# The second expert table of a PEER decoder layer in whole rows: 128 blocks of 8 KB per partition in place of 256 half rows, and two decode gather slots in place of three

## The chip, the cores and the metric

One core of one Trainium2 chip runs the kernel in one launch. The metric is the device time of one execution in microseconds (us); lower is better.

## The reference, cut to what matters

One decoder layer is computed for 256 prompt tokens (one sequence) and 64 decode tokens (8 sequences of 8), model width 2048, all in float32. Input projection, dilated attention and a short convolution, output projection and a layer norm come first. Then comes the part that the change touches, the PEER expert mixer: for each token, 8 heads choose 16 experts each out of 16384, and each expert is one row of 2048 floats in two tables, `peer_u` and `peer_v`.

```python
u = u_tab[et]                                    # (tokens, 128, 2048)
h = einsum('nd,nkd->nk', xt, u)
a = gt * gelu(h)                                 # gates from a softmax over the 16 scores
y = einsum('nk,nkd->nd', a, v_tab[et])
h = layer_norm(ALPHA * h + y)                    # ln2, then a gated per-layer embedding is added
```

## The kernel before, in words

Every engine has its own program, and semaphores order them. The stages are: input projection; attention and cache copies; output projection; query projection and expert selection (VectorE, "DVE"); the first expert table, one gathered row per prompt token and expert, 256 gathers of 128 rows (POOL issues them at L474, DVE multiplies and sums at L1102); building of the gate matrix; then the **second-table stage**, which the change rewrites; then layer norm 2, the gate projection and the output.

**The prompt's share of the second table is dense.** The gate matrix `gm` holds, for each of the 256 prompt tokens, a weight for each of the 16384 experts (zero for most), as 128 groups of 128 experts. So all of `peer_v` (128 MB) is streamed and multiplied: for group k, 128 rows of the table are a matrix of 128 x 2048, and the product with the 128 x 256 weights of the group is summed in PSUM over all 128 groups. To keep float32 precision both factors are split into a high part (rounded to fp32r) and a low part (the rest), and three matmuls are made of each product: hi x hi, hi x lo, lo x hi (`split_mm`, L1249 to L1251).

One group is worked in two pieces of 1024 columns (`PIECES = 256`, piece m = 2k + h):

- SP loads the piece into one of RL = 5 raw slots of 4 KB per partition (L427). It waits until PE has finished piece m - 5 (`vd_used`).
- ScalarE (ACT) makes the high part of the group's weights once per group (L688), then that of the piece (L694), in one of HS = 3 slots; it waits for piece m - 3 to be finished.
- DVE makes the low parts: of the weights once per group (L1181), of the piece (L1183), in place in the raw slot.
- PE makes 12 matmuls of 128x128 by 128x512 for the piece (2 token tiles x 2 column chunks x 3), so 24 per group, 3072 in all.

**The decode tokens' share is gathered beside it.** 64 decode tokens with two packed halves of their experts fill 128 partitions, so there are 64 gathers of the first table and 64 of the second, 1 MB each (8 KB per partition). POOL issues them (`decode_row`, L482) into DSLOT = 3 slots; a gather waits until DVE has used the slot (`d_free`). DVE uses one gather with one instruction over 128x2048 ("decode op" below): L1162 for the first table (a dot product), L1171 for the second (multiply and add). An order written out by hand says after which piece a decode op stands in DVE's program: `U_AT` puts op i behind piece 2i (64 ops over pieces 0 to 126, one per group), `W_AT` puts op 64 + i behind piece 134 + (27 i) // 16 (64 ops over pieces 134 to 240, 16 ops in 27 pieces).

```python
U_AT = {2 * i: i for i in range(64)}
W_AT = {134 + (27 * i) // 16: 64 + i for i in range(64)}
```

Memory: the gathers' slots lie at 152, 160 and 168 KB, the raw slots at 136 to 152 KB and 176 KB, the high slots at 180 to 192 KB. Near the end (m = 250) SP waits for the last decode op and loads the tokens back for the second layer norm: `x_tokens_again` (152 to 176 KB), one half MB folded from the decode sums and one load of 2 MB (L431). After the loop SP waits for `al_ok` (the last weights' low part) and loads the layer norm's gain and bias, two pieces of the gate weights and the embedding weights. In the code below the lines are those of the profile.

Of the kernel before, what the change touches and what calls it, by code (L numbers as in the profile page):

```python
# [35 lines left out]
DSLOT = 3  # L36
PAIRS = PH * TOPK
HALF = D // 2
EG = 4
GROUPS = 2 * 128 // EG  # L40
PIECES = 2 * NK
RL, HS, ST = 5, 3, 3
# [11 lines left out]
def decoder_step(nc, x_p, x_s, st_k, st_v, k_old, k_last, v_old, v_last, st_c, p_p, p_s, w_in, w_conv, w_out, ln1_g, ln1_b,  # L54
# [89 lines left out]
    ring = [at(f"expert_rows{i}", [128, D], f32, (152 if i < DSLOT else 96 - 24) * KB + i * 8 * KB) for i in range(NSLOT)]  # L144
# [3 lines left out]
    vrl = [at(f"v_raw{i}", [128, HALF], f32, (136 + 4 * i if i < 4 else 176) * KB) for i in range(RL)]  # L148
    vlo = [at(f"v_lo{i}", [128, HALF], f32r, (136 + 4 * i if i < 4 else 176) * KB) for i in range(RL)]
    vhi = [at(f"v_hi{i}", [128, HALF], f32r, (180 + 4 * i) * KB) for i in range(HS)]  # L150
# [76 lines left out]
    with ctx:  # L227
# [77 lines left out]
        GELU_AT = 130  # L305
# [5 lines left out]
        def _(sp):  # L311
# [104 lines left out]
            v_rows = v_tab.rearrange("(k p) (h c) -> p k h c", p=128, h=2)  # L416
# [22 lines left out]
            sp.wait_ge(vd_used, PIECES)  # L439
# [15 lines left out]
        def _(pool):  # L455
# [32 lines left out]
            for m in range(PIECES):  # L488
                if m in DECODE_AT and DECODE_AT[m] + DSLOT < 128:
                    decode_row(DECODE_AT[m] + DSLOT)  # L490
            pool.wait_ge(vd_used, PIECES)
# [5 lines left out]
        def _(act):  # L497
# [183 lines left out]
            for m in range(PIECES):  # L681
                k = m // 2
                if m == GELU_AT:
                    dots_gelu(2, 0, 64)
                if m % 2 == 0:
                    if k >= ST:
                        act.wait_ge(vd_used, 2 * (k - ST) + 2)
                    A(ghs[:, k % ST, :], gm[:, :, k], ACT.Copy).then_inc(ah_ok, 1)  # L688
                if m >= HS:
                    act.wait_ge(vd_used, m - HS + 1)  # L690
                act.wait_ge(v_raw[m % RL], 16 * (m // RL + 1))
                if m == 0:
                    act.wait_ge(u_free, 2 * PAIRS)
# [950 lines left out]
```

## Time and profile before

| | us |
|---|---|
| median of 3 runs | 2732.8 (2731.06 to 2736.54) |
| the profiled execution, its own time | 2726.47 |
| its span in the trace | 2724.7 |
| second-table stage, first to last matmul | about 1752 to 2508 |
| PE / DVE / ACT / POOL busy over the span | 1833.4 / 1781.7 / 770.8 / 1162.0 |

Times in the profile count from the start of the span. "Busy" of an engine leaves out waits and the issuing of DMAs. "DMA share" is the mean busy share of the core's 16 DMA engines. "PEclk" is the granted TensorE clock as a share of 2.4 GHz: 1.00 or 0.50. "us to landing" counts from the instruction that issues a transfer to the last byte's semaphore. An idle time is put down to the instruction that ended it.

### The profile page before, as it was taken

The numbers are of one execution on the slowest core, as the hardware profiler recorded it, in microseconds if no ns is written. First come the engines' busy times: TensorE is split into PE (matmuls) and PEld (weight loads), VectorE is DVE, ScalarE is ACT, GpSimd is POOL, SyncE is SP. The second block draws the span as 40 slices with busy tenths as digits, with TensorE's granted clock in tenths as the row PEclk, the third lists the DMA queues.
The fourth block names the chain that finished last, engine by engine and source line by source line (L and its number), as shares of the span: only waits on it lengthen the run. The fifth ranks groups of instructions, "written<-read, shape, count | busy, mean of one in ns | idle before, by whom it ended". The sixth has DMA issues, their size and how long they took to land.

```text
span 2724.7 us, 25002 instructions
## 1 busy us (share of the span) xinstructions
PE 1833.4 (67%) x9414; PEld 1467.2 (54%) x9414; DVE 1781.7 (65%) x2609; ACT 770.8 (28%) x1055; POOL 1162.0 (43%) x484
## 2 busy tenths in 40 slices
PE   7999995768969800000012222799999999997698
PEld 6889983335859800000011122677777777776476
DVE  1007155331141689999999999788888899996321
ACT  2222222112222200000012235644444444443222
POOL 4556640002535466677777676022222133220343
PEclk9999997878979955555555555999999999998799
DMA  9888975997687879999988899299999899997333
GB/s 326 321 332 325 375 287 245 407 428 322 253 315 274 311 308 368 376 389 401 421 342 343 335 364 374 80 364 360 358 372 353 330 381 393 390 377 249 124 132 123
DMA packets 124708, 880.59 MB, mean 323 GB/s; under 512 B 18402, under 2 KB 20002, under 8 KB 54980
## 3 DMA queue, kind: packets, MB, share of 16 engines
q1 hardware_dynamic: 69316, 476.65, 45.6%
q0 software_dynamic: 55296, 402.68, 37.3%
q8 instruction: 58, 0.95, 0.1%
q14 instruction: 38, 0.31, 0.0%
HBM read 870.76 MB, written 141.11 MB: 371 GB/s over the span
## 4 chain that ended last, share of the span: by engine, by line
issue 32%; DVE 27%; PE 22%; POOL 11%; DMA 7%; ACT 1%; POOLq 0%; DVEq 0%; ACTq 0%
DVE expert_rows L1102 15%; POOL w_lo L460 7%; PE psum L1249 7%; PE psum L1251 6%; PE psum L1250 6%; DMA v_raw<-in_peer_v 6%; POOL expert_rows L474 3%; DVE v_lo L1183 2%; DVE x_tokens L1171 2%; DVE one_hot_first_gated L1118 2%; PE psum L1476 1%; DMA expert_rows<-in_peer_u,experts 1%; DVE expert_rows L1162 1%; ACT v_hi L694 1%; PE psum L1538 1%
## 5 line engine op out<-in xcount | busy, mean ns | idle before, releaser
L474 POOL DMA_INDIRECT expert_rows<-in_peer_u,experts x256 | 521.0, 2035 | 230.8 <-DVE expert_rows L1102 115.9
L460 POOL TENSOR_TENSOR w_lo<-w_raw,w_hi 128x2048 fp32r<-128x2048 f32 x80 | 373.5, 4669 | 554.3 <-ACT w_hi L505 554.3
L1102 DVE SCALAR_TENSOR_TENSOR expert_rows<-expert_rows,x_tokens 128x2048 f32<-128x2048 f32 x256 | 572.1, 2285 | 12.7 <-DMA expert_rows<-in_peer_u,experts 12.1
L1249 PE MATMUL psum<-v_hi,gate_matrix_hi 128*128 128x512 f32 x1024 | 411.7, 402 | 25.6 <-DVE v_lo L1183 25.0
L1250 PE MATMUL psum<-v_lo,gate_matrix_hi 128*128 128x512 f32 x1024 | 405.6, 396 | 0.0
L1251 PE MATMUL psum<-v_hi,gate_matrix_lo 128*128 128x512 f32 x1024 | 405.2, 396 | 0.0
L694 ACT ACTIVATE v_hi<-v_raw 128x1024 fp32r<-128x1024 f32 x256 | 271.4, 1061 | 408.8 <-DMA v_raw<-in_peer_v 320.8
L1183 DVE TENSOR_TENSOR v_lo<-v_raw,v_hi 128x1024 fp32r<-128x1024 f32 x256 | 312.2, 1221 | 95.2 <-ACT v_hi L694 94.8
L505 ACT ACTIVATE w_hi<-w_raw 128x2048 fp32r<-128x2048 f32 x80 | 153.1, 1916 | 440.8 <-PE psum L1251 406.1
L1249 PEld LDWEIGHTS psum<-v_hi,gate_matrix_hi 128*128 128x128 f32 x1024 | 192.5, 188 | 95.3 <-issue 28.9
L1476 PE MATMUL psum<-one_hot_first_gated,one_hot_second 128*128 128x128 f32 x384 | 87.1, 399 | 227.4 <-DVE one_hot_first_gated L1118 217.2
L482 POOL DMA_INDIRECT expert_rows<-in_peer_u,experts_decode_packed x64 | 94.6, 1478 | 330.5 <-DVE expert_rows L1162 323.3
L1251 PEld LDWEIGHTS psum<-v_hi,gate_matrix_lo 128*128 128x128 f32 x1024 | 192.7, 188 | 47.2
L1250 PEld LDWEIGHTS psum<-v_lo,gate_matrix_hi 128*128 128x128 f32 x1024 | 192.9, 188 | 43.8
L1476 PEld LDWEIGHTS psum<-one_hot_first_gated,one_hot_second 128*128 128x128 f32 x384 | 75.1, 291 | 239.4 <-DVE one_hot_first_gated L1118 226.8
L1249 PE MATMUL psum<-act_T_hi,w_hi 128*128 128x320 f32 x640 | 200.0, 313 | 5.6 <-POOL w_lo L460 4.2
L482 POOL DMA_INDIRECT expert_rows<-in_peer_v,experts_decode_packed x64 | 96.8, 1513 | 244.0 <-DVE x_tokens L1171 226.5
L1250 PE MATMUL psum<-act_T_lo,w_hi 128*128 128x320 f32 x640 | 198.3, 310 | 0.0
L1251 PE MATMUL psum<-act_T_hi,w_lo 128*128 128x320 f32 x640 | 198.2, 310 | 0.0
L1249 PE MATMUL psum<-w_hi,act_T_hi 128*128 128x512 f32 x480 | 188.3, 392 | 6.3 <-POOL w_lo L460 4.7
L1250 PE MATMUL psum<-w_lo,act_T_hi 128*128 128x512 f32 x480 | 188.0, 392 | 0.0
L1251 PE MATMUL psum<-w_hi,act_T_lo 128*128 128x512 f32 x480 | 187.9, 391 | 0.0
(283 smaller groups left out, 2847.5 us busy)
## 6 DMA issues: line engine op xcount, KB each, us to landing
v_raw<-in_peer_v SPq DMA_DIRECT2D x256, 512.0 KB, 7.3
out<-in_state_attn_k SPq DMA_DIRECT2D x64, 1020.0 KB, 9.2
out<-in_state_attn_v SPq DMA_DIRECT2D x64, 1020.0 KB, 8.3
w_raw<-in_w_in SPq DMA_DIRECT2D x48, 1024.0 KB, 6.0
old_keys_T<-in_k_old SPq DMA_DIRECT2D x8, 3072.0 KB, 18.4
values_old<-in_v_old SPq DMA_DIRECT2D x8, 3072.0 KB, 19.0
last_keys_T<-in_k_last SPq DMA_DIRECT2D x8, 2048.0 KB, 21.5
values_last<-in_v_last SPq DMA_DIRECT2D x8, 2048.0 KB, 21.5
```

The source lines that it names most:

```text
L460: nc.gpsimd.tensor_tensor(l_, r_, h_.bitcast(f32), ALU.subtract).then_inc(w_lo_ready, 1)
L474: pool.indirect_dma_start(ring[n % NSLOT][:, :], None, u_tab, bass.IndirectOffsetOnAxis(idx_p[:, n // PAIRS, n % PAIRS:n % PAIRS + 1], 0)) ...
L482: pool.indirect_dma_start(ring[i % DSLOT][:, :], None, u_tab if i < 64 else v_tab, bass.IndirectOffsetOnAxis(idx_d[:, i % 64:i % 64 + 1], ...
L505: A(bufs[1][:, slot, :, :], bufs[0][:, slot, :, :], ACT.Copy).then_inc(w_hi_ready, 1)
L694: A(vhi[m % HS][:, :], vrl[m % RL][:, :], ACT.Copy).then_inc(vh_ok, 1)
L1102: V.scalar_tensor_tensor(out=g, in0=g, scalar=1.0, in1=xt[:, t, :], op0=ALU.mult, op1=ALU.mult, accum_out=hdot[:, t, j:j + 1]).then_inc(u_ ...
L1118: m = V.tensor_scalar(emov[:, e, j, :], iota[:, :], eT[:, n, 0, c:c + 1], aT[:, c:c + 1], ALU.is_equal, ALU.mult)
L1183: V.tensor_tensor(vlo[m % RL][:, :], vrl[m % RL][:, :], vhi[m % HS][:, :].bitcast(f32), ALU.subtract).then_inc(vl_d, 1)
L1249: MM(out, lh, rh, start=start, stop=False)
L1250: MM(out, lh, rl, start=False, stop=False)
L1251: return MM(out, ll, rh, start=False, stop=stop)
L1476: m = MM(PS[:, g % 4, j * NK:(j + 1) * NK], second_one_hot(g, j), emov[:, g % 2, j, :], start=True, stop=True)
```

## The change

The second table is loaded and worked in 128 blocks of 128 whole rows (8 KB per partition). Raw slots: three of 8 KB at 136, 144 and 168 KB; high slots: two of 8 KB at 176 and 184 KB. The slot at 168 KB was the third decode gather slot, so the decode gathers have two. The order of the decode ops in DVE's program stays. The last tile of `x_tokens_again` shares its place with raw slot 2, so its load waits for block 125 to be used.

```diff
-DSLOT = 3
+DSLOT, USLOT = 2, 3
-RL, HS, ST = 5, 3, 3
+RL, HS, ST = 3, 2, 3
...
-    vrl = [at(f"v_raw{i}", [128, HALF], f32, (136 + 4 * i if i < 4 else 176) * KB) for i in range(RL)]
-    vhi = [at(f"v_hi{i}", [128, HALF], f32r, (180 + 4 * i) * KB) for i in range(HS)]
+    V_AT = (136, 144, 168)
+    vrl = [at(f"v_raw{i}", [128, D], f32, a * KB) for i, a in enumerate(V_AT)]
+    vhi = [at(f"v_hi{i}", [128, D], f32r, (176 + 8 * i) * KB) for i in range(HS)]
...
-        GELU_AT = 130
+        GELU_AT = 65
@@ SP
-            for m in range(PIECES):
-                if m == 0:
+            for k in range(NK):
+                if k == 0:
                     sp.wait_ge(u_free, 128)
-                if m == 2:
+                if k == 1:
                     sp.wait_ge(u_free, 256)
-                if m == 4:
-                    sp.wait_ge(ab_mm, GROUPS)
-                if m >= RL:
-                    sp.wait_ge(vd_used, m - RL + 1)
-                sp.dma_start(vrl[m % RL][:, :], v_rows[:, m // 2, m % 2, :]).then_inc(v_raw[m % RL], 16)
-                if m == 250:
+                if k >= RL:
+                    sp.wait_ge(vd_used, k - RL + 1)
+                sp.dma_start(vrl[k % RL][:, :], v_rows[:, k, :]).then_inc(v_raw[k % RL], 16)
+                if k == 125:
                     sp.wait_ge(d_free, 128)
                     sp.dma_start(xt2[0:TS, 0, :], ydec[TS:128, :]).then_inc(fold_in, 16)
-                    sp.dma_start(xt2[:, 1:3, :], yp_v).then_inc(x2_in, 16)
+                    sp.dma_start(xt2[:, 1, :], yp_v[:, 0, :]).then_inc(x2_in, 16)
+            sp.wait_ge(vd_used, NK - 2)
+            sp.dma_start(xt2[:, 2, :], yp_v[:, 1, :]).then_inc(x2_in, 16)
@@ ACT
+                if k >= HS:
+                    act.wait_ge(vd_used, k - HS + 1)
+                act.wait_ge(v_raw[k % RL], 16 * (k // RL + 1))
+                A(vhi[k % HS][:, :], vrl[k % RL][:, :], ACT.Copy).then_inc(vh_ok, 1)
@@ DVE
+                V.tensor_tensor(vlo[k % RL][:, :], vrl[k % RL][:, :],
+                                vhi[k % HS][:, :].bitcast(f32), ALU.subtract).then_inc(vl_d, 1)
+                for m in (2 * k, 2 * k + 1):
+                    if m in DECODE_AT:
+                        decode_op(DECODE_AT[m])
@@ PE
+            for k in range(NK):
+                pe.wait_ge(al_ok, k + 1)
+                pe.wait_ge(vl_d, k + 1)
+                for h in range(2):
...
                 i.then_inc(vd_used, 1)
```

The loop over h, token tile and column chunk issues the same 24 matmuls in the same order.

## Rows read from the trace of the kernel before

**Rows 1.** The page: span; busy tenths in 40 slices of some 68 us.

```profile
span 2724.7 us, 25002 instructions
...
PE   7999995768969800000012222799999999997698
...
DMA  9888975997687879999988899299999899997333
```

**Rows 2.** By stretch: PE, PEld, DVE, ACT, POOL busy; PEclk, DMA share, GB/s.

```profile
1800.00:2100.00 300.00, 293.33 (x1236) 229.42 (x1235) 260.50 (x258) 137.32 (x155) 73.13 (x51) 1.00 0.96 362
...
2140.00:2450.00 310.00, 297.58 (x1244) 229.85 (x1243) 288.42 (x218) 138.75 (x156) 93.29 (x61) 1.00 0.98 380
2450.00:2508.00 58.00, 55.14 (x228) 43.60 (x228) 32.93 (x31) 23.30 (x26) 0.00 (x0) 0.97 0.78 277
```

**Rows 3.** Groups of instructions, 1800 to 2100 us: busy, mean ns, idle before.

```profile
L1183 DVE TENSOR_TENSOR v_lo<-v_raw,v_hi 128x1024 fp32r<-128x1024 f32 x104 | 127.1, 1222 | 40.3 <-ACT v_hi L694 40.1
L1162 DVE SCALAR_TENSOR_TENSOR expert_rows<-expert_rows,x_tokens 128x2048 f32<-128x2048 f32 x51 | 116.5, 2285 | 0.0
L694 ACT ACTIVATE v_hi<-v_raw 128x1024 fp32r<-128x1024 f32 x103 | 109.2, 1061 | 162.4 <-DMA v_raw<-in_peer_v 144.1 <-PE psum L1251 18.1
...
L1181 DVE TENSOR_TENSOR gate_matrix_lo<-gate_matrix,gate_matrix_hi 128x256 fp32r<-128x256 f32 x52 | 31.7, 611 | 0.0
```

**Rows 4.** The same view, 2140 to 2450 us.

```profile
L1171 DVE SCALAR_TENSOR_TENSOR x_tokens<-expert_rows,dots,x_tokens 128x2048 f32<-128x2048 f32 x62 | 145.4, 2346 | 0.1
...
L482 POOL DMA_INDIRECT expert_rows<-in_peer_v,experts_decode_packed x61 | 93.3, 1529 | 232.2 <-DVE x_tokens L1171 226.5 <-issue 5.7
```

**Rows 5.** DMA queues and issues, 1800 to 2100 us; last: us to landing.

```profile
q1 hardware_dynamic: 14960, 54.48, 48.1%
q0 software_dynamic: 7420, 53.97, 47.8%
...
v_raw<-in_peer_v SPq DMA_DIRECT2D x103, 512.0 KB, 7.3
expert_rows<-in_peer_u,experts_decode_packed POOLq DMA_INDIRECT x51, 9.2
```

**Rows 6.** The same view, 2140 to 2450 us.

```profile
q0 software_dynamic: 8687, 63.30, 52.0%
q1 hardware_dynamic: 14952, 54.45, 45.8%
...
v_raw<-in_peer_v SPq DMA_DIRECT2D x104, 512.0 KB, 7.6
expert_rows<-in_peer_v,experts_decode_packed POOLq DMA_INDIRECT x61, 9.2
```

**Rows 7.** DMA issues, light traffic: whole span, 1684 to 1691, 2460 to 2500.

```profile
w_raw<-in_w_out SPq DMA_DIRECT2D x16, 1024.0 KB, 5.0
...
expert_rows<-in_peer_u,experts_decode_packed POOLq DMA_INDIRECT x2, 6.6
...
v_raw<-in_peer_v SPq DMA_DIRECT2D x11, 512.0 KB, 4.9
x_tokens_again<-out SPq DMA_DIRECT2D x1, 2048.0 KB, 11.9
```

**Rows 8.** Timeline of PE, 2487 to 2496 us.

```profile
2488.70 0.39 PE L1250 MATMUL psum<-v_lo,gate_matrix_hi 128*128 128x512 f32 x1
2488.94 0.40 PE L1251 MATMUL psum<-v_hi,gate_matrix_lo 128*128 128x512 f32 x1
2491.91 0.50 PE L1249 MATMUL psum<-v_hi,gate_matrix_hi 128*128 128x512 f32 x1 [2.58 <-DVE v_lo L1183]
```

**Rows 9.** Timelines of DVE, then POOL: start us, us, engine, line.

```profile
2164.56 2.35 DVE L1171 SCALAR_TENSOR_TENSOR x_tokens<-expert_rows,dots,x_tokens 128x2048 f32<-128x2048 f32 x1
...
2167.18 1.68 POOL L482 DMA_INDIRECT expert_rows<-in_peer_v,experts_decode_packed  x1 [2.94 <-DVE x_tokens L1171]
```

**Rows 10.** A group of the page: 128x2048 on ACT.

```profile
L505 ACT ACTIVATE w_hi<-w_raw 128x2048 fp32r<-128x2048 f32 x80 | 153.1, 1916 | 440.8 <-PE psum L1251 406.1
```

More of the change, by code:

```diff
@@ L143, in decoder_step @@
     tlo = at("act_T_lo", [128, KT, N], f32r, 172 * KB)
-    ring = [at(f"expert_rows{i}", [128, D], f32, (152 if i < DSLOT else 96 - 24) * KB + i * 8 * KB) for i in range(NSLOT)]
+    ring = [at(f"expert_rows{i}", [128, D], f32, (152 if i < USLOT else 96 - 24) * KB + i * 8 * KB) for i in range(NSLOT)]
     xt2 = at("x_tokens_again", [128, 3, D], f32, 152 * KB)
@@ L147, in decoder_step @@
     esta = at("one_hot_second", [128, 2, EG, NK], f32, 180 * KB)
-    vrl = [at(f"v_raw{i}", [128, HALF], f32, (136 + 4 * i if i < 4 else 176) * KB) for i in range(RL)]
-    vlo = [at(f"v_lo{i}", [128, HALF], f32r, (136 + 4 * i if i < 4 else 176) * KB) for i in range(RL)]
-    vhi = [at(f"v_hi{i}", [128, HALF], f32r, (180 + 4 * i) * KB) for i in range(HS)]
+    V_AT = (136, 144, 168)
+    vrl = [at(f"v_raw{i}", [128, D], f32, a * KB) for i, a in enumerate(V_AT)]
+    vlo = [at(f"v_lo{i}", [128, D], f32r, a * KB) for i, a in enumerate(V_AT)]
+    vhi = [at(f"v_hi{i}", [128, D], f32r, (176 + 8 * i) * KB) for i in range(HS)]
     S0 = 184 * KB
@@ L487, in _ @@
                 decode_row(i)
-            for m in range(PIECES):
+            for m in range(2 * NK):
                 if m in DECODE_AT and DECODE_AT[m] + DSLOT < 128:
                     decode_row(DECODE_AT[m] + DSLOT)
-            pool.wait_ge(vd_used, PIECES)
+            pool.wait_ge(vd_used, NK)
             pool.wait_ge(xd_ok, 1)
@@ L680, in _ @@
             act.wait_ge(pack_rd, 1)
-            for m in range(PIECES):
-                k = m // 2
-                if m == GELU_AT:
+            for k in range(NK):
+                if k == GELU_AT:
                     dots_gelu(2, 0, 64)
[L685 to L692, printed above, removed]
+                if k >= ST:
+                    act.wait_ge(vd_used, k - ST + 1)
+                A(ghs[:, k % ST, :], gm[:, :, k], ACT.Copy).then_inc(ah_ok, 1)
+                if k >= HS:
+                    act.wait_ge(vd_used, k - HS + 1)
+                act.wait_ge(v_raw[k % RL], 16 * (k // RL + 1))
+                if k == 0:
                     act.wait_ge(u_free, 2 * PAIRS)
-                A(vhi[m % HS][:, :], vrl[m % RL][:, :], ACT.Copy).then_inc(vh_ok, 1)
+                A(vhi[k % HS][:, :], vrl[k % RL][:, :], ACT.Copy).then_inc(vh_ok, 1)
             layer_norm_root(3)
@@ L1493, in _ @@
             pe.wait_ge(ev_d, builds_dve(GROUPS - 1))
[L1494 to L1504 removed]
+            for k in range(NK):
+                pe.wait_ge(al_ok, k + 1)
+                pe.wait_ge(vl_d, k + 1)
+                for h in range(2):
+                    for t in range(2):
+                        tc = slice(t * 128, (t + 1) * 128)
+                        for c in range(2):
+                            cc = slice((2 * h + c) * CW, (2 * h + c + 1) * CW)
+                            i = split_mm(PS[:, 4 * h + 2 * t + c, :], (ghs[:, k % ST, tc], gls[:, k % ST, tc]),
+                                         (vhi[k % HS][:, cc], vlo[k % RL][:, cc]), k == 0, k == NK - 1)
                 i.then_inc(vd_used, 1)
```

35 lines of the change are left out of this document (8 added, 27 removed).

## The prediction

> **What bounds the kernel now.** I read the slices of the page first [rows 1]: in slices 26 to 37, about 1750 to 2510 us, PE and the DMA engines are both busy at nine tenths or more. That is the second-table stage, the only one that the change touches. Then the stretches [rows 2]: with gathers of the first table beside it (call it stretch U, 1800 to 2100 us) PE is busy for 293.3 of 300 us and the DMA share is 0.96; with those of the second table (W, 2140 to 2450 us) 297.6 of 310 us and 0.98. A busy PE need not be at its peak, so I take its pace from the timeline: matmuls start 0.234 us apart when nothing is waited for [rows 8], so 24 take 5.61 us. The stage runs slower than that. In U there are 52 low parts of weights, one per group of 128 rows, in 300 us [rows 3]: 5.77 us a block. In W, 62 decode ops stand in 310 us [rows 4], 5.00 us each; with 16 ops in 27 half blocks, so 1.185 per block, that is 5.93 us a block.
>
> The groups say who is late: ACT's high copy L694 waits 144 us of 300 for the raw piece to land [rows 3], and the pieces take 7.3 us from issue to landing [rows 5]. Yet a piece's life in its slot is what decides. Five slots turn once in five pieces, 14.4 us at 5.77 a block. In that time a slot is loaded (7.3), copied (1.06), lowered (1.22) and multiplied (2.80): 12.4 us. Only 2 us are left for waiting. So the stage stands at three limits that lie close together: PE, the DMA engines and the number of slots.
>
> **Raw slots.** The change doubles the grain and keeps three slots, 24 KB in place of 20 KB. A slot now turns once in three blocks. In it stand: the load L; the high copy, 1.92 us for 128x2048 on ACT [rows 10]; the low part, 2.29 us, as a 128x2048 two-input op on DVE [rows 3]; the 24 matmuls, 5.61; some 0.5 us of semaphores and the last matmul's drain, my estimate; and DVE's delay w when it is in a decode op as the high part gets ready, between 0 and 2.29 [rows 3], which I take at 0.7 since DVE idles some of each block. Together 3 P = L + 11.0. Before, 5.1 of 14.4 us went to the work on a piece; now it is 9.8 of 16.8 (at PE's pace), and with semaphores and w what is left for L is 5.8 us, for twice the bytes.
>
> How long is L? From below: 1 MB loads with little beside them take 5.0 us [rows 7]. From above: a gather, also 1 MB, beside the table's stream takes 9.2 us [rows 5]. L = 5.0 gives P = 5.33, so PE's 5.61 decides; L = 9.2 gives 6.73. I take L = 6.8, P = 5.93: half a megabyte alone took 4.9 us [rows 7] and 7.3 beside the gathers [rows 5], a surcharge of 2.4, and with one block loading at a time, not up to five pieces, there are stretches in which a block has the wires to itself, so three quarters of it, 1.8, on 5.0. U has 64 blocks: 64 x (5.93 - 5.77) = **+10 us**.
>
> The Trainium skill, "DMA: Bandwidth & Descriptors", section "Bandwidth", speaks for the change: transfers of at least 1 MiB are wanted, since each pays a fixed cost of about 2 us. Its fit gives 3.2 us for 512 KB and 4.4 us for 1 MB; by it L would lie under 5.8 and U would go at PE's pace. The fixed part is paid beside other transfers here, and the wires' time per megabyte does not show it: for 512 KB pieces 0.481 x 300 us / 54.48 MB = 2.65 us, for gathers of 8 KB rows 0.478 x 300 / 53.97 = 2.66 [rows 5]; in W 2.61 and 2.55 [rows 6]. So 8 KB rows are worth 0 to 2% of the table's half of the traffic, nothing in the sum.
>
> **Two gather slots.** A gather is issued 2.62 us after the start of the decode op that frees its slot (2164.56 to 2167.18) [rows 9], and lands G later. With s slots, s intervals must hold G + 2.6. With three and G = 9.2 an interval of 3.93 us is enough, under the 5.00 of W. With two, 2 x 5.00 = 10.0 is not enough for 9.2 + 2.6 = 11.8. From above, then, the interval is 5.90. From below, G = 6.6 with the wires free [rows 7] gives 4.60, less than PE and DVE need. G falls when less is in flight, and as the interval grows: per decode op the wires carry one gather (2.55 us per MB, 2.67 us) and 0.844 of a block (2.61 per MB, 2.31 us), 4.98 us, so at 5.5 they are busy for 0.91. At that share I put G nearer to the loaded row: 8.4, interval (8.4 + 2.6) / 2 = 5.5. There are 63 intervals: 63 x (5.5 - 5.0) = **+32 us**. DVE stands in the decode op while it waits, and behind it in its program stand the low part of the weights and that of the next block, so PE waits too: a block of W takes 1.185 x 5.5 = 6.5 us, 0.9 of it PE's idle time. At that period the raw slots are no limit (3 x 6.5 = 19.5 against 17.8). In U two intervals of 5.93 hold 11.9, just enough for G = 9.2, so the gathers cost nothing of their own there.
>
> **High slots, two in place of three.** ACT may start block k when PE has finished k - 2: 1.92 + 2.29 + 0.5 fits in 5.61 with 0.9 to spare, so DVE is at most that far ahead. Ten blocks of W carry two decode ops (groups 67, 72, 77, ... 115): 2.29 + 0.61 + 2 x 2.35 = 7.6 us of DVE's work in a block of 5.61. At 6.5 us a block this hides in the wait for the gathers; at PE's pace it would cost about 0.7 us each, 7 us.
>
> **Start and end.** PE's first matmul comes after one high copy and one low part: (1.92 - 1.06) + (2.29 - 1.22) = **+2 us**. The load that waited for the last build no longer does; three blocks are there beforehand, and the builds themselves decide. At the end, SP puts the 2 MB of tokens in front of the last pieces. One matmul waits 2.6 us for that [rows 8], and a granted clock of 0.97 over 58 us [rows 2] is 1.7 us more. Now only 1.5 MB go between blocks 125 and 126 and the rest after the last block: **-4 us**. The last 1 MB is issued two blocks (11.2 us) before the end, the 2 MB one took 11.9 us [rows 7], so it is hidden; the gain and bias behind it start some 3 us later and are needed 5 us after the last matmul, hidden too. If not, 2 us at most. The 256 instructions saved on ACT and DVE (0.2 and 0.16 us a block) lie beside waits and count nothing.
>
> **Sum:** 10 + 32 + 2 - 4 = +40 us. On the profiled execution, 2726.5 + 40 = 2766.5; it ran 6.3 us under the median of 2732.8, so I forecast a median of **2772 us**. Main case, 2745 to 2815 us.
>
> **Rivals.**
> - *Faster.* Block and gather take turns on the wires and hardly meet: L at most 5.8, G at most 6.9. Then U runs at PE's pace, 64 x (5.61 - 5.77) = -10, W at 5.61 / 1.185 = 4.73 per op, 63 x -0.27 = -17, the double blocks +7, start and end -2: -22, **2711 us**. For it: one block and one gather of 1.05 MB need 5.4 to 5.6 us of wires in 5.61. Against: that is a share of 0.96 to 0.99, with nothing left for a late one. It shows a gain from L under 6.4 and G under 7.4 on. The Trainium skill, same page, "Queues, rings and completion order", has each DMA engine alternate between queues packet by packet; if a row is a packet, the table's 8 KB rows get half of the wires where 4 KB rows got a third, which helps L and hurts G. No row here shows the interleaving.
> - *Slots decide outright.* Deep contention, L = G = 9.2: U 64 x (6.73 - 5.77) = +61, W 63 x 0.9 = +57, with the rest +116, **2849 us**. For it: 9.2 is what a loaded gather takes now. Against: less is in flight afterwards.
> - *Nothing.* L = 6.4 and G = 7.4: U stays at 5.8 us a block, W at 5.0 an op, 2733 us.
>
> **Chances.** Main case 0.58, faster 0.16, slots outright 0.16, nothing 0.10. A measurement of this kernel tells about 0.2%, 5.5 us, from no change. Faster 0.16, same 0.10, slower 0.74. The range leaves out the last tenth of either side: 2718 to 2835 us.
>
> **What the profile after should show.** Gathers: POOL waits as before, but DVE's decode ops now wait for "DMA expert_rows", some 0.5 to 1 us each in W and almost none in U; time to landing near 8.4 us. W from first to last decode op near 346 us (315 now). Landing of the 1 MB blocks near 6.8 us and ACT waiting for them. PE's idle time in W near 50 us, put down to DVE. DMA share about 0.9 in W. The granted clock stays at 1.00 in both stretches; if waits of PE brought it to 0.50 in them, the sum would be too small. I am wrong if decode ops in W do not wait for their gathers (faster), or if U's blocks take over 6.3 us (slots outright).

## The result, and the profile after

| us | before | after |
|---|---|---|
| median of the runs that were compared | 2731.93 (2730.06 to 2736.54, 4 runs) | **2781.23** (2779.19 to 2786.01, 4 runs) |
| ratio to before | | **1.018**, 95% interval 1.0161 to 1.020 |
| the profiled execution, its own time | 2726.47 | 2786.01 |
| its span | 2724.7 | 2784.2 |

The change makes the kernel 49 us slower; 2772 was forecast, inside 2718 to 2835. The two profiled executions lie 59.5 us apart, since the one of after is 4.8 us above its median and the one of before 5.5 below. The working by places below adds up to those 59.5.

**By stretch.** The same four stretches of the kernel after, with the columns of [rows 2] (the last one covers the end of the stage, which has moved):

```profile
1800.00:2100.00 300.00, 284.22 (x1188) 223.33 (x1189) 251.51 (x201) 124.10 (x101) 51.40 (x50) 0.99 0.95 348
2140.00:2450.00 310.00, 269.95 (x1083) 210.91 (x1082) 245.55 (x146) 112.77 (x92) 61.66 (x51) 0.94 0.89 324
2450.00:2508.00 58.00, 50.73 (x203) 39.33 (x202) 47.83 (x28) 19.86 (x16) 10.82 (x11) 0.94 0.90 333
2508.00:2565.00 57.00, 54.86 (x234) 43.32 (x233) 33.90 (x22) 23.03 (x18) 1.04 (x1) 1.00 0.77 273
```

Beside [rows 2], U (1800 to 2100 us) has lost a little of everything: PE is busy for 284 us where it was for 293. W (2140 to 2450 us) has lost much: 270 where it was 298, the DMA share is down from 0.98 to 0.89, and TensorE's granted clock, which stood at 1.00, is at 0.94, a mixture of its two levels.

**Where the 59.5 us are.** The timeline of DVE gives the first and the last decode op of each table, that of PE the last matmul:

```profile
1752.02 2.28 DVE L1159 SCALAR_TENSOR_TENSOR expert_rows<-expert_rows,x_tokens 128x2048 f32<-128x2048 f32 x1
...
2131.76 2.29 DVE L1159 SCALAR_TENSOR_TENSOR expert_rows<-expert_rows,x_tokens 128x2048 f32<-128x2048 f32 x1
...
2157.20 2.35 DVE L1168 SCALAR_TENSOR_TENSOR x_tokens<-expert_rows,dots,x_tokens 128x2048 f32<-128x2048 f32 x1
...
2518.77 2.34 DVE L1168 SCALAR_TENSOR_TENSOR x_tokens<-expert_rows,dots,x_tokens 128x2048 f32<-128x2048 f32 x1
```

```profile
2567.34 0.39 PE L1247 MATMUL psum<-v_hi,gate_matrix_lo 128*128 128x512 f32 x1
```

Before, the same five stood at 1751.85, 2117.08, 2142.00, 2456.43 and 2507.32.

| us | before | after | difference | predicted |
|---|---|---|---|---|
| first op of the first table starts | 1751.85 | 1752.02 | +0.2 | +2 |
| first to last op of the first table (U) | 365.2 | 379.7 | **+14.5** | +10 |
| on to the first op of the second table | 24.9 | 25.4 | +0.5 | |
| first to last op of the second table (W) | 314.4 | 361.6 | **+47.1** | +32 |
| on to the start of the last matmul | 50.9 | 48.6 | -2.3 | -4 |
| the rest of the span | 217.4 | 216.9 | -0.5 | 0 |

**Who is late in U.** The groups of the kernel after, 1800 to 2100 us, and the transfers of the same stretch (columns as in [rows 3] and [rows 5]):

```profile
L1178 DVE TENSOR_TENSOR v_lo<-v_raw,v_hi 128x2048 fp32r<-128x2048 f32 x51 | 116.8, 2291 | 51.0 <-ACT v_hi L691 50.9
L1159 DVE SCALAR_TENSOR_TENSOR expert_rows<-expert_rows,x_tokens 128x2048 f32<-128x2048 f32 x50 | 114.3, 2285 | 0.3 <-DMA expert_rows<-in_peer_u,experts_decode_packed 0.3
L691 ACT ACTIVATE v_hi<-v_raw 128x2048 fp32r<-128x2048 f32 x50 | 95.9, 1918 | 175.9 <-DMA v_raw<-in_peer_v 149.1 <-PE psum L1247 26.8
```

```profile
q0 software_dynamic: 7194, 52.38, 47.6%
q1 hardware_dynamic: 7114, 51.78, 46.7%
...
v_raw<-in_peer_v SPq DMA_DIRECT2D x50, 1024.0 KB, 7.0
```

ACT waits for blocks, DVE for ACT, and no decode op waits for its gather: the chain is the raw slots'. A block lands 7.0 us after its issue, and the blocks are 6.01 us apart (groups 8 to 62, by their weights' low parts; 5.82 before). Three turns of 6.01 less 7.0 leave 11.0 us of work in a slot, the constant of the forecast.

**Who is late in W.** The chain of waits of the kernel after, 2140 to 2450 us: who waits for whom, us in total, times, longest. Two further lines are from the DMA view of the stretch.

```profile
ACT v_hi L691 <- DMA v_raw<-in_peer_v: 102.8, 27, 6.0
ACT v_hi L691 <- PE psum L1247: 97.2, 19, 9.9
...
PE psum L1245 <- DVE v_lo L1178: 40.1, 19, 5.4
DVE v_lo L1178 <- ACT v_hi L691: 34.8, 26, 3.5
DVE x_tokens L1168 <- DMA expert_rows<-in_peer_v,experts_decode_packed: 31.4, 18, 4.8
```

```profile
q0 software_dynamic: 7210, 52.49, 46.5%
q1 hardware_dynamic: 6564, 47.88, 42.0%
```

DVE now waits for gathers, as forecast, but not a little each time: 18 of 51 decode ops wait, 1.7 us on average and 4.8 at most (0.5 to 1 us each was forecast). PE waits 19 times, 2.1 us on average and 5.4 at most; in the same stretch of before it waited 12.2 us in 23 times, 1.2 at most. ACT is held both by blocks that land late and by PE.

**One of the bursts.** Timeline of DVE in the kernel after, around a block with two decode ops:

```profile
2225.72 2.35 DVE L1168 SCALAR_TENSOR_TENSOR x_tokens<-expert_rows,dots,x_tokens 128x2048 f32<-128x2048 f32 x1
2232.88 2.35 DVE L1168 SCALAR_TENSOR_TENSOR x_tokens<-expert_rows,dots,x_tokens 128x2048 f32<-128x2048 f32 x1 [4.81 <-DMA expert_rows<-in_peer_v,experts_decode_packed]
2235.15 0.58 DVE L1176 TENSOR_TENSOR gate_matrix_lo<-gate_matrix,gate_matrix_hi 128x256 fp32r<-128x256 f32 x1
2235.65 2.28 DVE L1178 TENSOR_TENSOR v_lo<-v_raw,v_hi 128x2048 fp32r<-128x2048 f32 x1
```

That of ACT, for the high part that the last of these ops needs:

```profile
2229.42 1.92 ACT L691 ACTIVATE v_hi<-v_raw 128x2048 fp32r<-128x2048 f32 x1 [5.38 <-DMA v_raw<-in_peer_v]
```

And that of PE, with what it waited for in brackets, then the stretches around it (PE, PEld, DVE, ACT, POOL busy; PEclk, DMA share, GB/s):

```profile
2238.08 0.77 PE L1245 MATMUL psum<-v_hi,gate_matrix_hi 128*128 128x512 f32 x1 [5.35 <-DVE v_lo L1178]
2238.64 0.63 PE L1246 MATMUL psum<-v_lo,gate_matrix_hi 128*128 128x512 f32 x1
2239.07 0.63 PE L1247 MATMUL psum<-v_hi,gate_matrix_lo 128*128 128x512 f32 x1
```

```profile
2225.00:2236.00 11.00, 7.73 (x34) 5.86 (x32) 6.19 (x5) 2.96 (x3) 1.43 (x2) 1.00 0.98 340
2236.00:2243.00 7.00, 4.92 (x15) 3.96 (x16) 6.91 (x4) 1.96 (x2) 1.51 (x2) 0.76 0.88 303
```

Two ops stand behind this block. The second one's gather went out at 2222.74 (the timeline of POOL) and is awaited until 2232.88. DVE stands still for 4.8 us. The high part of the next block, late itself since its raw block was, is ready at 2231.34, but DVE comes to its low part only at 2235.65, and PE has nothing for 5.35 us. When it starts again, its matmuls are 0.43 us apart where they were 0.234 [rows 8]: the clock has fallen to its lower level, and the stretch shows 0.76. Counted over PE's timeline from 2138 us to the end of the stage, by the distance from one matmul's start to the next: 12 distances are over 2 us ("gaps" below; before: 1) and hold 42.5 us beyond the usual 0.234, all distances over 0.5 us together 55.4 (before 18.6), and 71 matmuls start at half pace (before 12). At 0.193 us each these are 13.7 us against 2.3. Over the same work, from the first matmul of block 66 to the stage's last, the two kernels take 418.2 and 371.5 us: of these 46.7 us, 36.8 are more waiting and 11.0 slow clock. That is a count; no run takes the slow clock away alone.

**Where the gaps stand.** The ten blocks with two decode ops ("double blocks" below) are 67, 72, 77, 83, 88, 94, 99, 104, 110 and 115. PE's 12 gaps lie in front of the first matmul of blocks 68, 69, 73, 78, 84, 89, 95, 100, 105, 111, 116 and 126: behind each of the ten double blocks stands one.

### The profile page after: what moved, and what is told of

It is laid out like the page before. It is cut to its first block, busy times and chain, and to the rows that moved or that the text cites. A ratio compares the mean times of both kernels' runs of the same rounds, so it can differ in the third digit from the quotient of the medians.

```text
span 2784.2 us, 24492 instructions
## 1 busy us (share of the span) xinstructions
PE 1846.9 (66%) x9414; PEld 1480.3 (53%) x9414; DVE 1777.7 (64%) x2481; ACT 745.8 (27%) x927; POOL 1116.9 (40%) x484
## 4 chain that ended last, share of the span: by engine, by line
issue 31%; DVE 25%; PE 19%; POOL 11%; DMA 10%; ACT 2%; POOLq 0%; ACTq 0%; DVEq 0%
DVE expert_rows L1099 15%; POOL w_lo L459 7%; DMA v_raw<-in_peer_v 6%; PE psum L1245 6%; PE psum L1246 6%; PE psum L1247 6%; DMA expert_rows<-in_peer_v,experts_decode_packed 4%; POOL expert_rows L473 4%; DVE v_lo L1178 2%; ACT v_hi L691 2%; DVE x_tokens L1168 2%; DVE one_hot_first_gated L1115 2%; PE psum L1472 1%; DMA expert_rows<-in_peer_u,experts 1%; PE psum L1533 1%
## 5 line engine op out<-in xcount | busy, mean ns | idle before, releaser
L1245 PE MATMUL psum<-v_hi,gate_matrix_hi 128*128 128x512 f32 x1024 | 417.7, 408 | 72.1 <-DVE v_lo L1178 72.0
L1246 PE MATMUL psum<-v_lo,gate_matrix_hi 128*128 128x512 f32 x1024 | 412.6, 403 | 0.0
L1247 PE MATMUL psum<-v_hi,gate_matrix_lo 128*128 128x512 f32 x1024 | 411.7, 402 | 0.0
L691 ACT ACTIVATE v_hi<-v_raw 128x2048 fp32r<-128x2048 f32 x128 | 245.4, 1917 | 491.4 <-DMA v_raw<-in_peer_v 318.0
L1178 DVE TENSOR_TENSOR v_lo<-v_raw,v_hi 128x2048 fp32r<-128x2048 f32 x128 | 293.1, 2290 | 120.0 <-ACT v_hi L691 119.8
L481 POOL DMA_INDIRECT expert_rows<-in_peer_u,experts_decode_packed x64 | 68.3, 1068 | 375.1 <-DVE expert_rows L1159 368.2
L481 POOL DMA_INDIRECT expert_rows<-in_peer_v,experts_decode_packed x64 | 75.7, 1183 | 313.4 <-DVE x_tokens L1168 298.7
```

The source lines that it names most:

```text
L481: pool.indirect_dma_start(ring[i % DSLOT][:, :], None, u_tab if i < 64 else v_tab, bass.IndirectOffsetOnAxis(idx_d[:, i % 64:i % 64 + 1], ...
L691: A(vhi[k % HS][:, :], vrl[k % RL][:, :], ACT.Copy).then_inc(vh_ok, 1)
L1178: V.tensor_tensor(vlo[k % RL][:, :], vrl[k % RL][:, :], vhi[k % HS][:, :].bitcast(f32), ALU.subtract).then_inc(vl_d, 1)
L1245: MM(out, lh, rh, start=start, stop=False)
L1246: MM(out, lh, rl, start=False, stop=False)
L1247: return MM(out, ll, rh, start=False, stop=stop)
```

## The experiments

Ratios are to runs of the kernel before on the same chip, with 95% intervals. "Block" is the distance of the blocks in U (groups 8 to 62) and W (groups 68 to 119), taken from the weights' low parts; "gaps" are the distances of over 2 us from one matmul's start to the next, from 2138 us to the end of the stage (for e8 that is from block 44 on, for the others from 62 to 68 on); PEclk is that of 2140 to 2450 us. "Whole" is one 8 KB row per partition, "half" is 4 KB. The kernel before had medians of 2727.1 to 2732.4 us beside the runs, so the difference of two medians from different rounds is uncertain by some 5 us.

| kernel | median us | ratio | raw, high, gather slots | block U | block W | gaps | PEclk |
|---|---|---|---|---|---|---|---|
| before | 2731.93 | 1 | 5 half, 3 half, 3 | 5.82 | 5.92 | 1 | 1.00 |
| after | 2781.23 | 1.018 (1.0161 to 1.020) | 3 whole, 2 whole, 2 | 6.01 | 6.82 | 12 | 0.94 |
| e1_two_gathers | 2786.57 | 1.0196 (1.0175 to 1.0217) | 5 half, 3 half, 2 | 5.94 | 6.90 | 16 | 0.96 |
| e2_half_pieces | 2773.19 | 1.0161 (1.0138 to 1.0185) | 6 half, 4 half, 2 | 6.00 | 6.72 | 12 | 0.96 |
| e3_no_second_gathers | 2737.48 | 1.0012 (0.9994 to 1.003) | as after | 6.04 | 5.77 | 1 | 0.99 |
| e4_spread | 2757.09 | 1.0095 (1.0071 to 1.0119) | as after | 5.94 | 6.22 | 5 | 0.98 |
| e5_before_spread | 2726.48 | 0.9999 (0.9979 to 1.002) | as before | 5.77 | 5.83 | 1 | 1.00 |
| e6_split_loads | 2806.79 | 1.0303 (1.0261 to 1.0346) | as after | 6.21 | 6.86 | 17 | 0.96 |
| e7_half_spread | 2754.14 | 1.0111 (1.008 to 1.0142) | as e2 | 5.96 | 6.21 | 2 | 0.98 |
| e8_two_raw_slots | 3074.51 | 1.1282 (1.125 to 1.1314) | 2 whole, 2 whole, 3 | 8.55 | 8.52 | 50 | 0.89 |
| e9_whole_rows_three_gathers | 2768.01 | 1.0136 (1.0116 to 1.0155) | 3 whole, 2 whole, 3 | 6.02 | 6.36 | 9 | 0.96 |
| e12_four_raw_slots | 2755.24 | 1.0092 (1.0061 to 1.0123) | 4 whole, 2 whole, 2 | 5.65 | 6.65 | 11 | 0.95 |
| e13_three_high_slots | 2785.21 | 1.0191 (1.0152 to 1.023) | 3 whole, 3 whole, 2 | 6.13 | 6.68 | 13 | 0.95 |
| e10_reload_split | 2721.34 | 0.9972 (0.996 to 0.9984) | as before | 5.78 | 5.95 | 0 | 1.00 |

Theory A is the prediction's: the raw slots set U, the gather slots set W.

### The two gather slots alone

The kernel before with the third decode gather slot left unused:

```diff
-DSLOT = 3
+DSLOT, USLOT = 2, 3
```

(USLOT keeps the ring of the other gathers as it is.)

> The kernel before (half rows, five raw and three high slots) with two gather slots in place of three and nothing else. Theory A (the two gather slots set W): the loss in W stays, 63 decode ops at 5.6 to 5.8 us in place of 5.0, and U stays at 5.8 us a block: 2770 to 2780 us. Theory B (the coarse blocks with three raw and two high slots are what costs): 2732 to 2740 us, W at 5.0 us an op.

The whole loss is there without a single whole row: 1.0196, W at 6.90 us a block. The chain of waits, 2140 to 2450 us:

```profile
DVE x_tokens L1171 <- DMA expert_rows<-in_peer_v,experts_decode_packed: 54.5, 32, 3.1
PE psum L1249 <- DVE v_lo L1183: 41.0, 25, 3.6
```

and the issues of U, us to landing last:

```profile
v_raw<-in_peer_v SPq DMA_DIRECT2D x101, 512.0 KB, 6.9
expert_rows<-in_peer_u,experts_decode_packed POOLq DMA_INDIRECT x51, 9.3
```

W goes as theory A says. What it had not expected is U: 5.94 instead of 5.82, with 33 of 51 decode ops waiting for their gathers (40.3 us). It is the prediction's own formula, (9.3 + 2.6) / 2 = 5.95. Beside half rows in five slots, two gather slots are a limit in U too, at nearly the same height as three raw slots of 8 KB; the prediction saw that they are "just enough" at 5.93 and did not ask which of the two would be left if the other went. The formula holds with the landing time that the run shows and gives no floor of its own: with four whole raw slots (below) two gather slots held 5.65.

### The same bytes in half rows

The kernel before with the memory of the change: six raw slots and four high slots of 4 KB, two gather slots, the tokens' reload in two parts as in the change.

```diff
-DSLOT = 3
+DSLOT, USLOT = 2, 3
-RL, HS, ST = 5, 3, 3
+RL, HS, ST = 6, 4, 3
+    V_AT = (136, 140, 144, 148, 168, 172)
```

> Half rows as before, in the same 56 KB as the changed kernel: six raw slots and four high slots of 4 KB, two gather slots. Against the changed kernel only the grain differs. Theory A: U goes back to 5.8 us a block (-14 us against the changed kernel), W stays near 5.7 us an op: about 2765 us. Theory B: both stretches go back, 2735 to 2745 us.

1.0161 against the 1.018 of whole rows; the intervals overlap, so coarse or fine makes little difference once two gather slots are given. Whole rows are at any rate not faster. U did not go back to 5.8 us a block, as had been expected: it stands at 6.00, with 46.1 us of waits for gathers in 42 ops, as in the run before.

### No gathers in the second half

The changed kernel without the 64 gathers of the second table; the decode ops stay and work on what the slots hold. Left out is therefore the decode tokens' share of the second table.

```diff
-                if m in DECODE_AT and DECODE_AT[m] + DSLOT < 128:
+                if m in DECODE_AT and DECODE_AT[m] + DSLOT < 64:
...
-                dve.wait_ge(d_in[i % DSLOT], 16 * (i // DSLOT + 1))
+                if i < 64:
+                    dve.wait_ge(d_in[i % DSLOT], 16 * (i // DSLOT + 1))
```

> The changed kernel without the 64 gathers of the second table; DVE's decode ops stay and use what lies in the slots. Theory A: W loses its limit and goes at 5.7 us a block in place of 6.85, 54 blocks: about 2781 - 62 = 2719 us, the loads landing in some 5 us. Theory B: the blocks' own turn of the slots stays the limit, W over 6.3 us a block, above 2750 us.

W falls to 5.77 us a block, under the 5.92 of before, the clock is back at 0.99, and one gap of over 2 us is left. PE waits for DVE 9 times there, 9.3 us in all, so the work of the ten double blocks, 7.6 us of DVE's against 5.6 of PE's, costs little by itself. U stays at 6.04. The median was expected at 2719 us and is 2737: from the first matmul of block 66 to the last this execution is 54 us shorter than the changed kernel's (62 expected), but it comes to block 66 7 us later. With this, W's loss belongs to the gathers, their waits or their share of the wires.

### The decode ops spread out

The changed kernel with the second table's ops over blocks 64 to 124, one per block in place of 1.185 (three blocks carry two, not ten); the fold of the decode sums follows one block later.

```diff
-        W_AT = {134 + (27 * i) // 16: 64 + i for i in range(64)}
+        W_BLOCK = [64 + (61 * i) // 64 for i in range(64)]
+        W_AT = {2 * x + (i > 0 and W_BLOCK[i - 1] == x): 64 + i for i, x in enumerate(W_BLOCK)}
...
-                if k == 125:
+                if k == 126:
```

> The changed kernel with the second table's decode ops over blocks 64 to 124, so 3 blocks with two ops in place of 10; the fold of the decode sums moves one block later. Theory A: one op per block asks for 6.0 us an op, which two slots just hold; blocks at 6.05 us from 64 to 124: the stage 815 - 40, about 2740 us. Theory B (blocks set the pace wherever the ops stand): less than 15 us gained, 2766 us or more. Third theory, C: what costs in W are the blocks with two ops, whose wait of some 5 us halves TensorE's clock afterwards; then the gain is as A's and the granted clock in the stretch goes back from 0.94 to 0.99 or more.

It gives back about half of the loss: 1.0095 in place of 1.018. In W the blocks are 6.22 us apart, and the chain of waits has changed sides:

```profile
ACT v_hi L692 <- DMA v_raw<-in_peer_v: 148.0, 42, 6.1
...
PE psum L1246 <- DVE v_lo L1179: 23.6, 17, 5.4
DVE x_tokens L1169 <- DMA expert_rows<-in_peer_v,experts_decode_packed: 10.1, 7, 2.9
```

With 5.94 us for each gather instead of 5.74 (first to last op), DVE hardly waits for them (10 us instead of 31), and the block loads are late, as in U. The three double blocks of this order are 64, 84 and 104, and the three longest of the five gaps (5.5, 3.8 and 4.9 us) stand right behind them, at blocks 65, 85 and 105. The clock is back at 0.98, where 0.99 or more had been expected of theory C. More had been expected (40 us, it was 24): under the limit of the gather slots lay that of the raw slots.

### The same order in the kernel before

```diff
-        W_AT = {134 + (27 * i) // 16: 64 + i for i in range(64)}
+        W_BLOCK = [64 + (61 * i) // 64 for i in range(64)]
+        W_AT = {2 * x + (i > 0 and W_BLOCK[i - 1] == x): 64 + i for i, x in enumerate(W_BLOCK)}
```

> The kernel before (half rows, three gather slots) with the second table's decode ops spread over groups 64 to 124 and the fold three pieces later; no part of the change. Its W was held at 5.93 us a group by a DMA share of 0.98 while the wires were at 0.84 in the groups without ops. If that is the limit, blocks 64 to 124 go at 5.8 us and the kernel gains some 8 to 12 us: about 2722 us. If PE's pace and the slots decide whatever the ops do: 2732 us.

0.9999 (0.9979 to 1.002), with the fold three pieces later as well: with five half slots and three gathers the order is worth nothing measurable. What it gave above it gave by mending the change.

### Whole slots, loaded by half rows

The changed kernel, each block loaded as two transfers of 512 KB in rows of 4 KB; ACT waits for both.

```diff
-                sp.dma_start(vrl[k % RL][:, :], v_rows[:, k, :]).then_inc(v_raw[k % RL], 16)
+                for h in range(2):
+                    hc = slice(h * D // 2, (h + 1) * D // 2)
+                    sp.dma_start(vrl[k % RL][:, hc], v_rows[:, k, hc]).then_inc(v_raw[k % RL], 16)
```

> The changed kernel with each 1 MB block loaded by two DMAs of column halves, so 4 KB rows on the wires as before, all else the same. If the DMA engines alternate between queues row by row, the table then gets a smaller part of the wires beside a gather: landing of a block from 7.0 to about 8 us, U from 6.0 to 6.3 us a block, some 2795 us. If the size of the rows does not matter: 2781 us, landing unchanged.

1.0303 against 1.018, some 25 us more by the medians and 34 by the ratios, and in U 6.21 us a block (2795 us and 6.3 had been expected if the rows matter). The DMA queues there, with packets, MB and the share of the engines' time:

```profile
q1 hardware_dynamic: 13878, 50.54, 48.9%
q0 software_dynamic: 6917, 50.37, 44.7%
```

A megabyte of the table now costs 0.489 x 300 / 50.54 = 2.90 us of the wires, against 0.467 x 300 / 51.78 = 2.71 with whole rows, and the gather's has fallen a little (2.66, it was 2.73). So in the same slots one load of whole rows is worth something, while the prediction had the row size at nothing, because in the kernel before both kinds of rows cost the same per megabyte [rows 5]. What of the 25 us is the row size and what the second issue per block stays open, since the edit changes both. It is not the row size alone: the half rows of the two runs above with half slots cost 0.475 x 300 / 53.04 = 2.69 (e1) and 0.489 x 300 / 52.61 = 2.79 us (e2) per megabyte in U.

### Half rows and spread ops together

The kernel of the half rows above with the spread order (the fold one step later as well).

> Six raw and four high slots of half rows with two gather slots, and the second table's ops spread over groups 64 to 124: two gather slots with the finer grain and no crowded stretch. Theory A (interval of the ops over two slots): -24 us as the spread gave in the changed kernel, about 2750 us, W at 6.0 us an op with gather waits mostly gone. Still over the kernel before, since 2 slots hold no interval under about 5.8 us.

1.0111 (1.008 to 1.0142), with whole rows 1.0095 (1.0071 to 1.0119): the same. The gather waits are frequent and short here (50 us in 41, 3.0 at most), and only two gaps of PE are over 2 us. Both gaps stand behind double blocks again (84 and 104). Neither grain wins in this memory.

### Only two raw slots

Whole rows, two raw slots, two high slots and the third gather slot back in its place.

```diff
-DSLOT, USLOT = 2, 3
-RL, HS, ST = 3, 2, 3
+DSLOT, USLOT = 3, 3
+RL, HS, ST = 2, 2, 3
```

> Whole rows with three gather slots and only two raw slots (and two high slots). This tries the sum on the turn of the raw slots: 2 P = L + 11.0, with L = 7.0 as measured P = 9.0 us a block in U and in W, the stage 128 x 9.0 = 1152 us, the kernel about 3120 us. If a block's load does not really stand in series with its copies and matmuls, P stays under 7.5 us and the kernel under 2950 us.

The slot formula is stretched here to where the DMA engines are far from full (a share of 0.68 in U) and PE is too. 2P = L + 11.0 with the landing time of quiet wires:

```profile
v_raw<-in_peer_v SPq DMA_DIRECT2D x35, 1024.0 KB, 4.9
expert_rows<-in_peer_u,experts_decode_packed POOLq DMA_INDIRECT x35, 5.6
```

That gives (4.9 + 11.0) / 2 = 7.95, and 8.55 was measured in U as in W, so the work in a slot is 12.2 us. Of the extra 1.2 us, 0.7 are PE's at the lower clock (187 of its matmul starts from block 8 to 62 are at half pace, 35.9 us in 54 blocks; granted clock 0.89); the rest stays open. The expectation had taken 7.0 us for L and so 9.0 a block and 3120 us; with less in flight a block lands sooner. With three slots, at 0.99 in U, the constant held to a tenth.

### Whole rows with three gather slots

The changed kernel with a third gather slot, in 8 KB freed by leaving out the second-table share of the first 16 prompt tokens (their weights are zeros; all matmuls stay).

```diff
-DSLOT, USLOT = 2, 3
+DSLOT, USLOT = 3, 3
...
+    dring = ring[:2] + [at("third_decode_rows", [128, D], f32, 0)]
...
-                A(ghs[:, k % ST, :], gm[:, :, k], ACT.Copy).then_inc(ah_ok, 1)
+                A(ghs[:, k % ST, 16:256], gm[:, 16:256, k], ACT.Copy).then_inc(ah_ok, 1)
```

> The changed kernel (whole rows, three raw and two high slots) with a third gather slot of 8 KB, made by leaving the weights of the first 16 prompt tokens out of the product (their columns are zero; the same matmuls are made). So the blocks change alone. Theory A: U stays at 6.0 us a block since the turn of the raw slots sets it (+12 us against the kernel before), in W no decode op waits for its gather and a block takes 6.0 to 6.1 us in place of 5.9 (+7 us), nothing halves TensorE's clock for long: about 2750 us. Theory B' (whole rows cost nothing by themselves, two gather slots explain all): 2732 us, U at 5.8. Theory C' (the low clock and the bursts come from the blocks, not from the gathers): W stays over 6.6 us a block, 2770 us or more.

1.0136 (1.0116 to 1.0155), 38 us above before and only 13 below the changed kernel: theory A in its plain form had wanted about 2750. The gathers are out of the chain in W, and the blocks have taken their place (2140 to 2450 us):

```profile
ACT v_hi L694 <- DMA v_raw<-in_peer_v: 133.9, 33, 7.4
...
DVE v_lo L1183 <- ACT v_hi L694: 55.5, 23, 7.4
PE psum L1250 <- DVE v_lo L1183: 30.3, 21, 4.4
DVE x_tokens L1171 <- DMA expert_rows<-in_peer_v,experts_decode_packed: 0.6, 1, 0.6
```

Blocks are 6.36 us apart where the gathers do not matter, between the 6.1 of theory A and the 6.6 of theory C', so 3 x 6.36 = 19.1 us is what three raw slots take in W: 7.2 of landing (the median in this stretch) and 11.9 of work, 0.9 more than in U. Two decode ops in front of a low part (DVE's delay w in the forecast) and the slower clock would both make it longer; no run separates them. PE still has nine gaps, so whole rows in three slots bring some by themselves; but only one of them, at block 68, stands behind a double block. Two gather slots alone cost 54 us, three whole raw slots alone 38, both together 49. That the two do not add fits two limits of the same stretch at nearly the same height; it is a reading, not a test.

### The spare memory to a fourth raw slot

The same 8 KB (same tokens left out), two gather slots, but four raw slots.

```diff
-RL, HS, ST = 3, 2, 3
+RL, HS, ST = 4, 2, 3
-    V_AT = (136, 144, 168)
+    V_AT = (136, 144, 168, 0)
```

> The changed kernel with the spare 8 KB per partition of the three-gather-slot run given to the table instead: four raw slots of 8 KB, two high slots, two gather slots (weights of the first 16 prompt tokens left out, their zeros multiplied as before). Theory A (the two gather slots set W, the raw slots U): with four raw slots 4P = L + 12.2 is no limit, U falls from 6.0 to at most 5.85 us a block (-10 us), W keeps 5.75 us an op: 2765 to 2775 us. Rival C (the grain: with little held in reserve every double block drains PE, whoever is late): a block more in reserve carries PE over part of the ten bursts, but ACT and DVE can use it only as far as the two high slots let them, so W falls by at most 10 us: 2755 to 2770 us. Rival D (more loads in flight make the gathers slower): no gain or a loss, 2780 us or more, with the gathers' landing above 9.

1.0092 (1.0061 to 1.0123), 26 us less than the changed kernel, twice what the gather slot gave. U is the fastest of all, 5.65 us a block, close to PE's pace of 5.61; two intervals less the 2.6 of the issue leave 8.7 us for a gather, where 9.3 had been measured with two gather slots and half rows. Its windows, 1800 to 2100 and 2140 to 2450 us:

```profile
1800.00:2100.00 300.00, 297.81 (x1271) 236.96 (x1270) 266.18 (x213) 130.11 (x106) 53.52 (x53) 1.00 0.97 370
2140.00:2450.00 310.00, 272.47 (x1101) 214.85 (x1102) 255.03 (x150) 111.99 (x92) 61.82 (x56) 0.95 0.92 342
```

and the chain of waits in U:

```profile
ACT v_hi L694 <- PE psum L1252: 170.1, 53, 4.1
DVE expert_rows L1162 <- DMA expert_rows<-in_peer_u,experts_decode_packed: 27.4, 29, 2.5
...
PE psum L1250 <- DVE v_lo L1183: 2.1, 5, 0.8
```

ACT waits for PE and for nothing else. DVE waits 27 us for gathers, up to 2.5 at a time, and PE loses 2.1: while the blocks come early, a short wait of DVE stays hidden. U's loss is the raw slots', as forecast, and this run is 22 us under the changed kernel there (first to last op: 1752.03 to 2109.95, 357.9 us against 379.7). W gains less: its blocks are 6.65 us apart for 6.82, and first to last op take 352.9 us for 361.6, with 41 us of waits for gathers. Ten of its eleven gaps stand behind the ten double blocks. ACT waits for no block there, so W's first limit is the gather slots, as forecast.

### The spare memory to a third high slot

```diff
-RL, HS, ST = 3, 2, 3
+RL, HS, ST = 3, 3, 3
```

> The same with the spare 8 KB as a third high slot: three raw, three high and two gather slots (weights of the first 16 prompt tokens left out). As predicted (two high slots cost nothing, DVE in its program order is what is late in W): 2776 to 2786 us, no difference to the changed kernel. Rival C (with two high slots DVE is never more than 0.9 us ahead of PE, so every late op reaches PE): ACT and DVE can be a whole block ahead and PE rides over the double blocks: W 5.5 us an op or less, PE's waits over 2 us in W at most half of the changed kernel's twelve, 2755 us or less.

1.0191 (1.0152 to 1.023), as the changed kernel. Two high slots cost nothing that this run can show, as predicted. ACT and DVE could be a block further ahead, but ACT waits for raw blocks (186.8 us in 47 waits, 2140 to 2450 us), so it can't use it. 13 gaps are left, nine of them behind double blocks.

### The end of the change on the kernel before

Only the tokens' reload is taken over: one tile behind m = 250 as before, the second when PE has finished four pieces short of the end.

```diff
-                    sp.dma_start(xt2[:, 1:3, :], yp_v).then_inc(x2_in, 16)
+                    sp.dma_start(xt2[:, 1, :], yp_v[:, 0, :]).then_inc(x2_in, 16)
+            sp.wait_ge(vd_used, PIECES - 4)
+            sp.dma_start(xt2[:, 2, :], yp_v[:, 1, :]).then_inc(x2_in, 16)
```

> The kernel before with the end of the change alone: of the 2 MB of tokens loaded back, one tile stays in front of the last pieces and the other is loaded behind them. The prediction put 4 us on this (one wait of 2.6 us of a matmul and a stretch at half clock): expected 2728 us against 2732, the stage's last matmul 2 to 5 us nearer to the last decode op; nothing measurable in the median if the wait is met elsewhere.

0.9972 (0.996 to 0.9984): 2721.34 us, a small gain that is clear of the noise. SP's timeline shows the second tile's load behind the last pieces and ahead of the gain and bias:

```profile
2477.37 11.53 SPq L427 DMA_DIRECT2D v_raw<-in_peer_v  x5
2491.69 0.33 SPq L433 DMA_DIRECT2D x_tokens_again<-out  x1
2492.07 0.43 SPq L436 DMA_DIRECT2D ln_gain_bias<-in_ln_g  x1
```

From the last decode op (2455.7) to the end of the last matmul (2502.9) it takes 47.2 us, 51.3 before, and the granted clock over the stage (1752 to 2503 us) is 1.00. These 4.1 us are the prediction's last term, out of 4.9 us between the two profiled executions. The medians are 8.5 us apart (4.4 to 10.9 by the interval); where the rest comes from was not traced.

## Why the prediction was right or wrong

**Right: direction and places.** Slower by 49 us (+40 in the forecast), most of it in W, a fourth in U, a small gain at the end. The forecast of 2772 is 9 us low, and that is not noise. Most of its signs came as written: decode ops waiting for gathers in W and not in U (31.4 us against 0.3), landing of blocks at 7.0 us (6.8), DMA share 0.89 in W (0.9).

**Raw slots in U: right.** 3P = L + 11.0 with L = 7.0 gives 6.0, measured 6.01; +14.5 us from first to last op for +10. L was 0.2 us more, and the 5.77 of before, a count of 52 blocks in 300 us, is 5.82 by distance. Three raw slots with three gather slots give 6.02, so the term is the raw slots' here; four raw slots take it away.

**High slots: right**, by the run with a third one.

**Start and end: right in size.** The first low weights came 1.8 us earlier in this execution (1748.0, before 1749.8) and the first matmul 0.2 later, so the start costs the 2 us of the forecast. The end gave 2.3, and 4.1 when it was done alone.

**Two gather slots in W: right mechanism, wrong size: +47 for +32.** Of the 15 us too few, 11 are the slow clock, by the count above, and some 4 more waiting. So the sum of the waits was nearly right and their places were not. The failing step is the sentence that a block takes 1.185 x 5.5 us with "0.9 of it PE's idle time", and that the double blocks' work "hides in the wait for the gathers". It treats the interval (G + 2.6) / 2 as even. G was about as assumed: where an op of W waited (24 of 64), its gather had taken 8.3 us on average from issue to the op's start, which gives 5.5. But the second op of a double block waits for a gather that could go out only when the op two before it had freed the slot, and at other places DVE is held by ACT instead (34.8 us), while the gather is there: 33 of 51 ops did not wait. What a double block loses isn't won back then, and the interval came out at 5.74. The places of the gaps show it: in the changed kernel and with four raw slots one gap stands behind each of the ten double blocks (with half rows and two gather slots behind nine of them in e1, seven in e2); with three gather slots one of nine gaps does; without gathers there is one gap in all; and with the ops spread the longest gaps moved to the three double blocks of that order.

**The clock: wrong, though the condition stood there.** The forecast was 1.00 in both stretches, "if waits of PE brought it to 0.50 in them, the sum would be too small". They did. In the kernel before, waits of up to 1.2 us in W left the clock at 1.00; behind the bursts of 3 to 5 us here it fell. The Trainium skill, "TensorE: Matmul & The Clock Gate", section "HAM oscillation — how this bites in real kernels", describes kernels that wait for data and lose the clock besides; the rows at 2238 us agree (5.35 us of waiting, then starts 0.43 apart and a granted 0.76).

**The raw slots in W: too small.** "At that period the raw slots are no limit (3 x 6.5 = 19.5 against 17.8)" left 1.7 us a turn; with three gather slots the blocks still took 6.36 us, a turn of 19.1, so 0.4 was left. The second limit stood close under the first: giving back a gather slot takes W from 6.82 to 6.36 and not to the 5.92 of before.

**Row size: open, without effect on the sum.** In the same slots two loads of half rows in place of one of whole rows cost 25 us or more, but there the loads are twice as many as well; with the same memory in half slots (e2) the half rows cost nothing. The Trainium skill, "DMA: Bandwidth & Descriptors", section "Bandwidth", wants transfers of at least 1 MiB. This case agrees in the first comparison (2781 against 2807 us), and disagrees where the size is paid for with slots in flight: with three gather slots on both sides, five half slots give 2732 us and three whole ones 2768.

**The rivals.** "Faster" is out: L was 7.0, not under 6.4. "Slots decide outright" had U at 6.73 a block: out for U; in W its 5.90 an op was not far from 5.74, of which a part is the clock and not the landing. "Nothing" wanted L = 6.4, which was not reached.

## What to carry to other kernels

A transfer is held up by the number of slots that can be in flight and by how long work occupies a slot, so count 3P = L + work before trading slots for size; in the changed kernel 8 KB per partition was worth 26 us as a raw slot, 13 as a gather slot and nothing measurable as a high slot. Where several consumers in one engine's order share the reserve, look at the worst place of the order, not at its mean: a wait of up to 5 us at ten places of W cost PE the wait and the clock behind it, while 27 us of gather waits in 29 pieces, with the blocks early (U with four raw slots), cost PE 2 us. A part of a losing change can be a gain by itself, as the split reload was.

## What the runs showed of the hardware

- Landing times depend on what is in flight: 1 MB of the table took 4.9 us at a DMA share of 0.68, 7.0 at 0.95 and 7.6 with four raw slots at 0.97 (there blocks wait for PE, not PE for blocks); a gather of 1 MB 5.6 at 0.68 and 9.2 to 9.3 at 0.96.
- Two loads of 512 KB in 4 KB rows to one block took 2.90 us of the DMA engines per MB, one load in 8 KB rows 2.71. Half rows in half slots took 2.65 (before), 2.69 (e1) and 2.79 (e2), so the 4 KB row alone does not set it.
- After a pause of 5.35 us PE's 128x512 matmuls started 0.43 us apart instead of 0.234. In the run with two raw slots, with pauses up to 6.2 us, the granted clock was 0.89 over both stretches.
